# Two filler k-steps in each level of a triangular inverse, set apart (one core, two-layer hybrid encoder step)

## The chip, the cores and the metric

One core of a Trainium2 chip runs the whole program in one launch. The time is the device time of one execution in microseconds (us); the median of three executions is compared. TensorE (PE) multiplies, VectorE (DVE), ScalarE (ACT) and GpSimd (POOL) work beside it, and SyncE (SP) issues the transfers.

## What is computed

Two layers of a streaming encoder over 512 prompt frames and 32 frames of a running stream (544 columns), model width 1024. In each layer one projection of the normalised input gives the columns of three mixers and three gate blocks:

```python
xn = _rms_norm(x, P['norm_mix_pre'][l])
cols = jnp.einsum('btd,dc->btc', xn, P['w_in'][l]).astype(jnp.float32)
ca, cb, cc, cg = _split(cols, [A_COLS, B_COLS, C_COLS, N_BRANCH * D_MODEL])
...
merged = (gates[:, :, 0] * (h_a @ P['w_branch_a'][l])
          + gates[:, :, 1] * (h_b @ P['w_branch_b'][l])
          + gates[:, :, 2] * (h_c @ P['w_branch_c'][l]))
```

A is an mLSTM, B a sliding-window attention, C the RWKV-7 mixer with the recurrence

```python
S = (S * w[:, :, None, :]
     + jnp.einsum('bhij,bhj->bhi', S, -kk)[..., None] * (kk * a)[:, :, None, :]
     + v[..., None] * k[:, :, None, :])
```

A SwiGLU feed-forward layer of width 2816 follows. Everything is in float32.

## The kernel before

**Large products.** All projections are cut into units of 128 output columns (512 KB of weights each, fetched by SyncE into one of three slots). A weight is split into a high part (ScalarE, L1058) and a low part (GpSimd, L1979), the activations likewise, and a k-step of such a unit is three passes of two matmuls over 272 columns; eight k-steps make a unit. The `branch` units are not split: four k-steps of two float32 matmuls. `gate` and `branch` units stand in the plan in turn, eight of each for branch A and eight for branch B while mixer C runs.

**Mixer C** works in five groups: four of 128 frames (two chunks of 64 frames, 8 heads) and one of 32 frames. In each chunk the recurrence becomes matrix products with the inverse of a unit triangular matrix. `c_gram` makes the matrix (a_rb) and the first step of the inverse; then `c_level` doubles the size of the inverted diagonal blocks, five times for L = 64 (k = 1 to 5) and four times for L = 32. It keeps the inverse `inv` (it lies in the buffer `c_scratch`) and its transpose `invT` (in `c_kk`); `w_lev` lies in `c_in_rate`. A level on TensorE is made of these products, each of them 16 small matmuls 64 rows deep (8 of 32 rows in the last group; a float32 matmul leaves two records in the trace):

- W = a_rb times inv, into bank 1 (`psum_mixer<-c_scratch,c_a_rb` in the trace);
- B3, the update of inv, into bank 3 (`psum_mixer<-c_in_rate,c_kk`), left out in the last level;
- B2, the update of invT, into bank 2 (`psum_mixer<-c_kk,c_in_rate`).

VectorE masks W into w_lev (L1553), then subtracts B3 from inv and B2 from invT (both L1561). The waits: B3 needs the mask; the next level's W needs inv updated. `claim` is the wait of TensorE until a bank's last reader is done.

**Filler.** `fill(n)` puts up to n k-steps of the next large unit into TensorE's stream where it would otherwise wait; when the unit is used up it does nothing. The units themselves stand in the plan between the steps of C (`weave`), and take the k-steps that the fillers have left. The other engines walk through the same plan; when a branch product is complete, VectorE multiplies it by its gate and adds it to `merged` (L1764, L1766), in the plan's order, after the updates of the level before it. Every engine does its own list in order, and the order is fixed when the program is written.

The level as TensorE's function has it:

```python
by_head(1, a_rb[:, :, 0, :], inv, ("c_w", l, g, k))
fill(2)
bank[1].claim(pe)
if k < (5 if L == 64 else 4):
    by_head(3, invT, w_lev, ("c_inv", l, g, k))
by_head(2, w_lev, invT, ("c_invT", l, g, k))
```

Of the kernel before, what the change touches and what calls it, by code (L numbers as in the profile page):

```python
# [252 lines left out]
def build(nc, a, o):  # L253
# [166 lines left out]
    with ctx:  # L420
# [29 lines left out]
        def flow(name):  # L450
            if name not in flows:
                flows[name] = count(name)
            return flows[name]
# [87 lines left out]
        def c_group(g):  # L541
            return (P, P * g, 2, 64) if g < 4 else (TS, TP + 1, 1, TS)
# [14 lines left out]
        def _(pe):  # L557
            def mm(out, lhsT, rhs, start=True, stop=True):
                return pe.matmul(out, lhsT, rhs, start=start, stop=stop, skip_group_check=True)  # L559
# [49 lines left out]
            def product(s, steps=8):  # L609

                kind = s[0]
                if kind == "branch":
                    l, b, m = s[1:]
                    rhs = [(acols[:, AQ + k, :], bh[:, k, :], cc[:, k, :])[b] for k in range(4)]
                    gemm(s, rhs=rhs, nk=4, steps=steps)
                else:
                    gemm(s, rh=xh, rl=xl, cut=SPLIT_C if kind == "cols_c" or (kind == "cols_b" and s[2] < 4) else HALF,
                         wait_k=bool(first_user.get("norm")), steps=steps)
                    first_user["norm"] = False

            def fill(steps):

                if unit_at[0] < len(units):
                    s = units[unit_at[0]]
                    if (s[0] in ("cols_b", "cols_c", "gate") or (s[0] == "cols_a" and 12 <= s[2] < 16)
                            or (s[0] == "branch" and s[3] > 0)):
                        product(s, steps)
# [96 lines left out]
            def pairs(c):  # L724

                for p in range(4):
                    for q in range(2):
                        yield 4 * c + p, p, slice(64 * q, 64 * q + 64), slice(64 * q, 64 * q + c_rows[0])
# [31 lines left out]
            def c_level(l, g, k):  # L760


                n, at, nch, L = c_group(g)

                def by_head(b, lhsT, rhs, mark=None):
                    bank[b].claim(pe)
                    for c in range(nch):
                        for i, p, dims, rows in pairs(c):
                            last = mm(mp[b][rows, i * L:(i + 1) * L], lhsT[rows, i, 0:L], rhs[rows, i, 0:L])
                    bank[b].filled(last, "dve", mark)  # L770

                if k == 1:
                    flow("c_inv0").wait_next(pe, "pe")
                else:
                    bank[3].wait_emptied(pe, ("c_inv", l, g, k - 1))
                by_head(1, a_rb[:, :, 0, :], inv, ("c_w", l, g, k))
                fill(2)
                bank[1].claim(pe)
                if k < (5 if L == 64 else 4):
                    by_head(3, invT, w_lev, ("c_inv", l, g, k))  # L780
                by_head(2, w_lev, invT, ("c_invT", l, g, k))

            def c_chain(l, g, c):
# [218 lines left out]
            for s in plan:  # L1002
# [22 lines left out]
                elif kind == "merge_split":  # L1025
                    pass
                elif kind == "mix":
                    gemm(s, rh=xh, rl=xl, wait_k=s[2] == 0)
                elif kind == "ffn_out":
                    l, m, q = s[1:]  # L1030
                    if m == 0 and q == 0:
                        flow("hidden").wait_next(pe, "pe", KF)
                    gemm(s, rh=hid_h, rl=hid_l, k0=8 * q, nk=nk_of(s), first=q == 0, last=q == 2)
                elif kind == "c_shift_out":
                    c_shift_out()
                elif kind == "store_y":
                    pe.wait_ge(flow("x_new").sem, KD * DEPTH)
                    pe.wait_ge(flow("x_new_odd").sem, KD * DEPTH)
                    store_y()
                else:  # L1040
                    {"c_prep": c_prep, "c_gram": c_gram, "c_level": c_level, "c_chain": c_chain, "c_finish": c_finish,
                     "c_state_out": c_state_out, "c_gate_in": lambda l: None, "c_rsqrt": lambda l: None,
                     "c_variance": c_variance,
                     "c_keys": c_keys, "c_scale": c_keys, "c_scaled": c_scaled, "a_norm": lambda l: None,
                     "a_rows": lambda l: None, "a_rows_exp": lambda l: None, "a_rows_put": lambda l: None,
                     "a_rows_get": lambda l: None, "a_scale": lambda l: None, "a_chunk": a_chunk,
                     "a_chunk_out": a_chunk_out, "a_out": a_out, "b_values": b_values, "b_scores": b_scores,
                     "b_out": b_out}[kind](*s[1:])
# [991 lines left out]
```

How the kernel before makes its waits and increments, by code:

```python
    def wait_next(self, eng, who, n=1):  # L120
        self.seen[who] = self.seen.get(who, 0) + n
        eng.wait_ge(self.sem, self.seen[who])
# [8 lines left out]
    def __call__(self, ins, count=None):  # L132
        c = count or self.chain
        c.inc(ins)
        self.eng.wait_ge(c.sem, c.value)
# [12 lines left out]
    def claim(self, pe):  # L148
        if self.last:
            pe.wait_ge(self.empty[self.last].sem, self.full[self.last].value)
# [9 lines left out]
    def wait_emptied(self, eng, mark):  # L161
        eng.wait_ge(*self.marks[mark])
# [397 lines left out]
            def order_after(ins):  # L561
                chains["pe"].inc(ins)
                pe.wait_ge(chains["pe"].sem, chains["pe"].value)
# [3 lines left out]
            def gemm(s, rh=None, rl=None, rhs=None, first=True, last=True, cut=HALF, wait_k=False, k0=0, nk=8, steps=8):  # L568
# [1 line left out]
                ks = range(done_k.get(s, 0), min(nk, done_k.get(s, 0) + steps))
                if not ks:
                    return
                done_k[s] = ks[-1] + 1
                key = s[:3] if s[0] == "ffn_out" else s
                pair, reader, turn = tiles[key]
                if s in split_no:
                    slot = split_no[s] % NSPLIT
                    if ks[0] == 0:
                        pe.wait_ge(low_ready.sem, split_no[s] + 1)
                else:
                    at, value = landed_at[s]
                    slot = unit_no[s] % NRAW
                    if ks[0] == 0:
                        pe.wait_ge(landed[at].sem, value)
                if first and ks[0] == 0 and tile_no[key] >= 2:
```

## Time and profile before

| what | value |
|---|---|
| runs | 2665.5, 2658.36, 2649.56 us, median 2658.36 |
| profiled execution | 2656.14 us; its span, first to last instruction, 2654.4 us |
| PE busy | 2406.3 us (91%), 23176 instructions |
| PE weight loads busy | 2255.5 us (85%) |
| DVE, ACT, POOL busy | 881.6, 845.9, 732.2 us |
| mean granted TensorE clock | 0.952 |
| levels of layer 0 and of layer 1 | between 414 and 723 us, and between 1720 and 2023 us |

The span runs from the first to the last instruction of one execution; the profiled execution's own time is 1.7 us longer. A share of an engine is busy time; the chain of waits tells which busy time set the end. Timeline rows give a start, a duration, the engine, the line (for all small and large products here the helper's line L559), the operation with output and inputs, and how many records are merged; in brackets the idle time before it and who ended it. Durations of matmuls overlap, so that the length of a step is read as the distance from its start to the next step's start.

### The profile page before, as it was taken

How to read it: one execution, taken by the hardware profiler on the slowest of the kernel's cores; microseconds unless marked ns; L12 is line 12 of the kernel's file. 1: busy time of each engine (PE TensorE's matmuls, PEld its weight loads, DVE VectorE, ACT ScalarE, POOL GpSimd, SP SyncE). 2: the span in 40 equal slices, each digit the busy share in tenths (PEclk: the TensorE clock that was granted, in tenths of full speed). 3: DMA queues.
4: the chain of work that ended last, by engine and by line, in shares of the span. 5: the costliest groups of instructions: out<-in, count | busy, mean ns of one | idle time of the engine just before them, and what ended most of it. 6: DMA issues, size and time to landing. Idle time of an engine off the chain costs nothing.

```text
span 2654.4 us, 51984 instructions
## 1 busy us (share of the span) xinstructions
PE 2406.3 (91%) x23176; PEld 2255.5 (85%) x23176; DVE 881.6 (33%) x1394; ACT 845.9 (32%) x1408; POOL 732.2 (28%) x330
## 2 busy tenths in 40 slices
PE   4998898999899799999979889999998988999996
PEld 3997887888798699999969878888887987999996
DVE  2232654554333411110042346454343324111102
ACT  3343441222242422222243344322213243222222
POOL 1321221111122334443333222211102133444342
PEclk9997899999999899999989989999999997999998
DMA  5423210111123133322234231111112131333231
GB/s 153 122 52 68 56 45 26 38 38 37 43 62 117 40 88 88 88 86 80 74 94 118 44 72 49 41 38 38 38 28 63 56 122 40 88 88 88 82 88 56
DMA packets 335447, 181.35 MB, mean 68 GB/s; under 512 B 35512, under 2 KB 332456, under 8 KB 334072
## 3 DMA queue, kind: packets, MB, share of 16 engines
q1 hardware_dynamic: 335224, 178.03, 24.0%
q8 instruction: 183, 3.00, 0.5%
q14 instruction: 40, 0.33, 0.0%
HBM read 168.62 MB, written 9.38 MB: 67 GB/s over the span
## 4 chain that ended last, share of the span: by engine, by line
PE 76%; DVE 9%; ACT 6%; DMA 4%; issue 3%; POOL 2%; SPq 1%; DVEq 0%; ACTq 0%; POOLq 0%
PE psum_products L559 60%; PE psum_mixer L559 15%; DMA w_raw<-in_w_in 2%; POOL w_low L1979 1%; ACT w_high L1058 1%; DVE squares L1422 1%; SPq L1834 1%; DVE x L1438 1%; DMA w_raw<-in_w_out 1%; ACT L1058 1%; DVE squares L1435 1%; DVE squares_ffn L1435 1%; ACT b_scores_even L1058 1%; DMA bias_skewed<-bias_line 0%; DVE a_dexp L1655 0%
## 5 line engine op out<-in xcount | busy, mean ns | idle before, releaser
L1979 POOL TENSOR_TENSOR w_low<-w_raw,w_high 128x1024 fp32r<-128x1024 f32 (+1 forms) x274 | 659.7, 2408 | 1715.9 <-ACT w_high L1058 1715.7
L559 PE MATMUL psum_products<-xn_high,w_high 128*128 128x272 f32 (+2 forms) x3616 | 793.0, 301 | 83.1 <-POOL w_low L1979 38.9
L559 PE MATMUL psum_products<-xn_high,w_low 128*128 128x272 f32 (+2 forms) x3616 | 763.5, 293 | 0.0
L559 PE MATMUL psum_products<-xn_low,w_high 128*128 128x272 f32 (+2 forms) x3616 | 762.5, 293 | 0.0
L559 PEld LDWEIGHTS psum_products<-xn_high,w_high 128*128 128x128 f32 x3616 | 586.4, 194 | 112.2 <-POOL w_low L1979 54.1
L559 PEld LDWEIGHTS psum_products<-xn_low,w_high 128*128 128x128 f32 x3616 | 587.9, 194 | 0.0
L559 PEld LDWEIGHTS psum_products<-xn_high,w_low 128*128 128x128 f32 x3616 | 583.4, 194 | 0.0
L1058 ACT ACTIVATE w_high<-w_raw 128x1024 fp32r<-128x1024 f32 (+1 forms) x274 | 286.5, 1046 | 255.3 <-PE psum_products L559 144.9
L559 PE MATMUL psum_products<-hidden_high,w_high 128*128 128x272 f32 x704 | 147.4, 291 | 4.8 <-DVE hidden_low L1770 4.8
L559 PE MATMUL psum_products<-hidden_low,w_high 128*128 128x272 f32 x704 | 146.4, 289 | 0.0
L559 PE MATMUL psum_products<-hidden_high,w_low 128*128 128x272 f32 x704 | 145.8, 289 | 0.0
L1796 DVE SCALAR_TENSOR_TENSOR ffn_product<-ffn_tanh,psum_products 128x544 f32<-128x544 f32 x44 | 31.7, 721 | 256.9 <-ACT ffn_tanh L1058 256.9
L559 PEld LDWEIGHTS psum_products<-hidden_high,w_high 128*128 128x128 f32 x704 | 111.6, 191 | 5.2 <-DVE hidden_low L1770 5.2
L559 PEld LDWEIGHTS psum_products<-hidden_low,w_high 128*128 128x128 f32 x704 | 111.8, 190 | 0.0
L559 PEld LDWEIGHTS psum_products<-hidden_high,w_low 128*128 128x128 f32 x704 | 111.1, 190 | 0.0
L1058 ACT ACTIVATE hidden_high<-ffn_product 128x544 fp32r<-128x544 f32 x44 | 29.0, 658 | 228.1 <-DVE ffn_product L1803 228.1
L1058 ACT ACT_TABLE_LOAD x69 | 88.5, 1283 | 33.6 <-PE psum_products L559 25.1
L1058 ACT ACTIVATE gate_tanh<-psum_products 128x544 f32<-128x544 f32 x32 | 19.9, 623 | 245.2 <-PE psum_products L559 245.1
L1817 DVE TENSOR_TENSOR squares_ffn<-squares_ffn 128x544 f32<-128x544 f32 x14 | 10.2, 725 | 262.1 <-ACT squares_ffn L1058 262.1
L1803 DVE SCALAR_TENSOR_TENSOR ffn_product<-ffn_product,psum_products 128x544 f32<-128x544 f32 x44 | 31.7, 721 | 174.9 <-PE psum_products L559 174.9
L1655 DVE SCALAR_TENSOR_TENSOR a_dexp<-a_g_spread,a_cols_tokens,consts 128x128 f32<-128x128 f32 (+1 forms) x40 | 31.1, 778 | 150.6 <-ACT stats L1058 149.6
L1058 ACT ACTIVATE ffn_tanh<-psum_products 128x544 f32<-128x544 f32 x44 | 27.5, 624 | 150.1 <-PE psum_products L559 150.1
(311 smaller groups left out, 2643.1 us busy)
## 6 DMA issues: line engine op xcount, KB each, us to landing
w_raw<-in_w_in SPq DMA_DIRECT2D x112, 512.0 KB, 3.8
w_raw<-in_w_ffn_in SPq DMA_DIRECT2D x88, 512.0 KB, 3.7
w_raw<-in_w_ffn_out SPq DMA_DIRECT2D x32, 512.0 KB, 3.4
w_raw<-in_w_out SPq DMA_DIRECT2D x16, 512.0 KB, 3.6
w_raw<-in_w_ffn_out SPq DMA_DIRECT2D x16, 384.0 KB, 3.0
x_kept<-x SPq DMA_DIRECT2D x2, 2176.0 KB, 7.8
x<-x_kept SPq DMA_DIRECT2D x2, 2176.0 KB, 8.5
w_raw<-in_w_in SPq DMA_DIRECT2D x16, 256.0 KB, 3.2
```

What stands on the lines that cost most here:

```text
L559: return pe.matmul(out, lhsT, rhs, start=start, stop=stop, skip_group_check=True)
L1058: return act.activation(out, in_, f, **kw_)
L1422: step(stt(out=squares[:, k, :], in0=x[:, k, :], scalar=prm[:, l, g0 + k:g0 + k + 1], in1=rstd[:], op0=MUL, op1=MUL), xn_part)
L1435: step(stt(out=tmp[:, k, :], in0=src[:, k, :], scalar=prm[:, l, g0 + k:g0 + k + 1], in1=rstd[:], op0=MUL, op1=MUL), flow("x_step_odd") if ...
L1438: step(tt(x[:, k, :], x[:, k, :], tmp[:, k, :], ADD), flow("x_new"))
L1655: step(stt(out=dexp[0:n, h * n:(h + 1) * n], in0=g_all[0:n, h, at:at + n], scalar=a_cols_t[0:n, g, h:h + 1], in1=C("future_neg")[0:n, 0:n] ...
L1796: step(stt(out=halves(ffn_p[:, j % 2, :]), in0=halves(ffn_t[:, j % 2, :]), scalar=1.0, in1=pair_view(pair), op0=ADD, op1=MUL), emptied["dve"])
L1803: step(stt(out=halves(ffn_p[:, j % 2, :]), in0=halves(ffn_p[:, j % 2, :]), scalar=0.5, in1=pair_view(pair), op0=MUL, op1=MUL), emptied["dve"])
L1817: step(tt(sq[:, 0, :], sq[:, 0, :], sq[:, m, :], ADD), flow("squares_added") if m == KD - 1 else None)
L1834: c.inc(sp.dma_start(dst, src), 16)
L1979: low_ready.inc(pool.tensor_tensor(wl[:, n % NSPLIT, 0:nk], wraw[:, slot, 0:nk], wh[:, n % NSPLIT, 0:nk].bitcast(F32), ALU.subtract))
```

## The change

In `c_level` on TensorE the two k-steps no longer stand together behind W: one stays there, the other goes between B3 and B2. The wait for bank 1 (the mask) stays between the first k-step and B3; in the last level, which has no B3, it now stands between the two k-steps.

```diff
@@ -774,10 +774,11 @@
                 else:
                     bank[3].wait_emptied(pe, ("c_inv", l, g, k - 1))
                 by_head(1, a_rb[:, :, 0, :], inv, ("c_w", l, g, k))
-                fill(2)
+                fill(1)
                 bank[1].claim(pe)
                 if k < (5 if L == 64 else 4):
                     by_head(3, invT, w_lev, ("c_inv", l, g, k))
+                fill(1)
                 by_head(2, w_lev, invT, ("c_invT", l, g, k))
```

The order of the other four engines is the same, row for row. Per layer there are 24 levels: in 16 the filler is parted (the 13 at full width are 7 with gate k-steps and 6 with branch k-steps; the 3 of the 32-frame group have gate k-steps), in 5 (the last of each group) the wait falls between the two k-steps, and in 3 the unit is used up and there is no filler.

TensorE's order, group 0 of layer 0, first level; the filler is a gate unit (`psum_products<-xn_high,w_high` and its two companions). Before:

```order
L559 MATMUL psum_mixer<-c_scratch,c_a_rb 64x64 [waits bank1_emptied_by_dve,c_inv0]
L559 MATMUL psum_mixer<-c_scratch,c_a_rb 64x64 x15
L559 MATMUL psum_products<-xn_high,w_high 128x272 x2
L559 MATMUL psum_products<-xn_low,w_high 128x272 x2
L559 MATMUL psum_products<-xn_high,w_low 128x272 x2
L559 MATMUL psum_products<-xn_high,w_high 128x272 x2
L559 MATMUL psum_products<-xn_low,w_high 128x272 x2
L559 MATMUL psum_products<-xn_high,w_low 128x272 x2
L559 MATMUL psum_mixer<-c_in_rate,c_kk 64x64 [waits bank3_emptied_by_dve,bank1_emptied_by_dve]
L559 MATMUL psum_mixer<-c_in_rate,c_kk 64x64 x15
L559 MATMUL psum_mixer<-c_kk,c_in_rate 64x64 [waits bank2_emptied_by_dve]
L559 MATMUL psum_mixer<-c_kk,c_in_rate 64x64 x15
```

The same place in the changed kernel:

```order
L559 MATMUL psum_mixer<-c_scratch,c_a_rb 64x64 [waits bank1_emptied_by_dve,c_inv0]
L559 MATMUL psum_mixer<-c_scratch,c_a_rb 64x64 x15
L559 MATMUL psum_products<-xn_high,w_high 128x272 x2
L559 MATMUL psum_products<-xn_low,w_high 128x272 x2
L559 MATMUL psum_products<-xn_high,w_low 128x272 x2
L559 MATMUL psum_mixer<-c_in_rate,c_kk 64x64 [waits bank3_emptied_by_dve,bank1_emptied_by_dve]
L559 MATMUL psum_mixer<-c_in_rate,c_kk 64x64 x15
L559 MATMUL psum_products<-xn_high,w_high 128x272 x2
L559 MATMUL psum_products<-xn_low,w_high 128x272 x2
L559 MATMUL psum_products<-xn_high,w_low 128x272 x2
L559 MATMUL psum_mixer<-c_kk,c_in_rate 64x64 [waits bank2_emptied_by_dve]
L559 MATMUL psum_mixer<-c_kk,c_in_rate 64x64 x15
```

Three rows (six matmuls, one k-step) have moved from ahead of B3 to behind it. The last level of the same group, before:

```order
L559 MATMUL psum_products<-xn_high,w_high 128x272 [waits products_emptied_by_act,w_low_ready]
L559 MATMUL psum_products<-xn_high,w_high 128x272
L559 MATMUL psum_products<-xn_low,w_high 128x272 x2
L559 MATMUL psum_products<-xn_high,w_low 128x272 x2
L559 MATMUL psum_products<-xn_high,w_high 128x272 x2
L559 MATMUL psum_products<-xn_low,w_high 128x272 x2
L559 MATMUL psum_products<-xn_high,w_low 128x272 x2
L559 MATMUL psum_mixer<-c_kk,c_in_rate 64x64 [waits bank2_emptied_by_dve,bank1_emptied_by_dve]
```

And in the changed kernel:

```order
L559 MATMUL psum_products<-xn_high,w_high 128x272 [waits products_emptied_by_act,w_low_ready]
L559 MATMUL psum_products<-xn_high,w_high 128x272
L559 MATMUL psum_products<-xn_low,w_high 128x272 x2
L559 MATMUL psum_products<-xn_high,w_low 128x272 x2
L559 MATMUL psum_products<-xn_high,w_high 128x272 [waits bank1_emptied_by_dve]
L559 MATMUL psum_products<-xn_high,w_high 128x272
L559 MATMUL psum_products<-xn_low,w_high 128x272 x2
L559 MATMUL psum_products<-xn_high,w_low 128x272 x2
L559 MATMUL psum_mixer<-c_kk,c_in_rate 64x64 [waits bank2_emptied_by_dve]
```

Here no matmul has moved; the wait for the mask has moved ahead of the second k-step.

## Rows read from the trace of the kernel before

**Rows 1.** Chain of waits, shares of the span by line

```profile
PE psum_products L559 60%; PE psum_mixer L559 15%; DMA w_raw<-in_w_in 2%; POOL w_low L1979 1%; ACT w_high L1058 1%; DVE squares L1422 1%; SPq L1834 1%; DVE x L1438 1%; DMA w_raw<-in_w_out 1%; ACT L1058 1%; DVE squares L1435 1%; DVE squares_ffn L1435 1%; ACT b_scores_even L1058 1%; DMA bias_skewed<-bias_line 0%; DVE a_dexp L1655 0%
```

**Rows 2.** Windows: length, busy PE, PEld, DVE, ACT, POOL; PEclk; DMA share; GB/s

```profile
380.00:720.00 340.00, 312.67 (x4926) 278.30 (x4925) 154.63 (x255) 90.66 (x154) 48.72 (x25) 0.97 0.14 39
1680.00:2040.00 360.00, 332.94 (x5181) 295.54 (x5180) 164.24 (x277) 95.99 (x163) 52.80 (x27) 0.97 0.15 39
414.00:440.00 26.00, 24.59 (x520) 22.01 (x518) 10.39 (x16) 1.68 (x2) 2.35 (x1) 1.00 0.12 33
```

**Rows 3.** Timeline, group 0, first level, gate filler: start, length, engine, operation

```profile
414.31 1.15 PE L559 MATMUL psum_mixer<-c_scratch,c_a_rb 64*64 64x64 f32 x32
415.39 0.52 PE L559 MATMUL psum_products<-xn_high,w_high 128*128 128x272 f32 x2
415.58 0.69 DVE L1553 TENSOR_TENSOR c_in_rate<-psum_mixer,consts 128x512 f32<-128x512 f32 x1 [1.92 <-PE psum_mixer L559]
...
417.09 1.15 PE L559 MATMUL psum_mixer<-c_in_rate,c_kk 64*64 64x64 f32 x32
...
419.10 0.52 PE L559 MATMUL psum_products<-xn_high,w_high 128*128 128x272 f32 x2
...
420.80 1.15 PE L559 MATMUL psum_mixer<-c_scratch,c_a_rb 64*64 64x64 f32 x32
```

**Rows 4.** Timeline, group 0, second level, branch filler, up to the next W

```profile
423.91 1.15 PE L559 MATMUL psum_mixer<-c_in_rate,c_kk 64*64 64x64 f32 x32
424.89 1.10 PE L559 MATMUL psum_mixer<-c_kk,c_in_rate 64*64 64x64 f32 x32
425.18 0.69 DVE L1561 TENSOR_TENSOR c_scratch<-c_scratch,psum_mixer 128x512 f32<-128x512 f32 x1 [2.42 <-PE psum_mixer L559]
425.92 1.15 PE L559 MATMUL psum_mixer<-c_scratch,c_a_rb 64*64 64x64 f32 x32
```

**Rows 5.** Timeline of c_gram: one k-step alone, gate and branch

```profile
409.02 0.52 PE L559 MATMUL psum_products<-xn_high,w_high 128*128 128x272 f32 x2
...
409.97 1.96 PE L559 MATMUL psum_mixer<-c_kappa_r,c_kprime 64*64 64x128 f32 x32
...
633.16 1.19 PE L559 MATMUL psum_products<-b_heads,w_raw 128*128 128x272 f32 x4
...
634.27 1.96 PE L559 MATMUL psum_mixer<-c_kappa_r,c_kprime 64*64 64x128 f32 x32
```

**Rows 6.** Timeline, group 0, fourth level, no filler left

```profile
431.04 1.15 PE L559 MATMUL psum_mixer<-c_scratch,c_a_rb 64*64 64x64 f32 x32
...
433.05 1.15 PE L559 MATMUL psum_mixer<-c_in_rate,c_kk 64*64 64x64 f32 x32 [0.86 <-DVE c_in_rate L1553]
```

**Rows 7.** Timeline, group 1, fourth level, two merge operations ahead of the mask

```profile
505.79 1.15 PE L559 MATMUL psum_mixer<-c_scratch,c_a_rb 64*64 64x64 f32 x32
...
506.70 0.72 DVE L1764 SCALAR_TENSOR_TENSOR gate_product<-gate_tanh,psum_products 128x544 f32<-128x544 f32 x1
...
508.21 0.69 DVE L1553 TENSOR_TENSOR c_in_rate<-psum_mixer,consts 128x512 f32<-128x512 f32 x1
508.96 1.15 PE L559 MATMUL psum_mixer<-c_in_rate,c_kk 64*64 64x64 f32 x32 [0.33 <-DVE c_in_rate L1553]
```

**Rows 8.** Timeline, group 0, last level: W and its mask

```profile
435.06 1.15 PE L559 MATMUL psum_mixer<-c_scratch,c_a_rb 64*64 64x64 f32 x32
...
436.73 0.69 DVE L1553 TENSOR_TENSOR c_in_rate<-psum_mixer,consts 128x512 f32<-128x512 f32 x1
```

**Rows 9.** Timeline, group 4 (32 frames): B3, next W, its mask, next B3

```profile
713.84 0.44 PE L559 MATMUL psum_mixer<-c_in_rate,c_kk 32*32 32x32 f32 x16
...
715.05 0.44 PE L559 MATMUL psum_mixer<-c_scratch,c_a_rb 32*32 32x32 f32 x16 [0.52 <-DVE c_scratch L1561]
...
715.66 0.60 DVE L1553 TENSOR_TENSOR c_in_rate<-psum_mixer,consts 32x128 f32<-32x128 f32 x2
...
717.12 0.44 PE L559 MATMUL psum_mixer<-c_in_rate,c_kk 32*32 32x32 f32 x16
```

## The prediction

> **What bounds the kernel now.** I read the chain of waits first, then the windows over the two stretches in which the levels run, then the timeline of single levels. The chain ends in TensorE for three quarters of the span: matmuls into psum_products 60%, into psum_mixer 15% [rows 1]. So whatever lengthens TensorE's own stream there lengthens the kernel, unless a wait that is timed by something else absorbs it. In both stretches TensorE is busy 92% of the time at a mean granted clock of 0.97, and inside the levels at 1.00 [rows 2].
>
> A level has three products, called W, B3 and B2 here (banks 1, 3, 2). On VectorE a mask follows W, and the updates of inv and invT follow B3 and B2. The timeline of group 0 gives all prices of a full-width level [rows 3, 4]:
> - W holds TensorE 1.08 us when filler follows (414.31 to 415.39).
> - Two gate k-steps in one piece take 1.70 (415.39 to 417.09); two branch k-steps 2.03 (3.11 from 420.80 to 423.91, less 1.08).
> - B3 takes 0.98 when B2 follows (423.91 to 424.89), and B2 1.03; together 2.01, from B3 to the next W or to the next product.
> - The inv update ends at 425.87, 0.05 before W at 425.92. By its spacing W could have come some 0.1 earlier, so this is the whole wait that a filler between B3 and B2 can hide at full width.
> - The first wait is the larger one. Where no filler is left, B3 comes 2.01 after W, 0.86 of it idle until the mask is done [rows 6]. With one k-step of filler W's side is 1.08 + 0.95 = 2.03: it just covers the mask. The second k-step is spare there, which is the case for moving it.
>
> **What the change costs.** No instruction is added or removed; VectorE, ScalarE, GpSimd and the DMA queue keep their order. On TensorE one of two k-steps moves from ahead of B3 to behind it in 16 levels of a layer (13 at full width, 3 in the narrow group 4). In the five last levels, which have no B3, both k-steps stay together and the wait for the mask is now ahead of the second. In three levels the filler has run out and nothing changes.
>
> A split filler is dearer than a whole one. A single gate k-step between two small products takes 0.95 (409.02 to 409.97), a single branch k-step 1.11 (633.16 to 634.27) [rows 5]. So two apart cost 1.90 against 1.70, or 2.22 against 2.03, and B3, now followed by filler, 1.08 instead of 0.98: 0.30 us for each place where 64-row and 128-row matmuls alternate once more. The Trainium skill (TensorEngine Tiling (Array Packing), Key Properties) says that going to another tiling mode drains the engine, while another tile of the same mode doesn't; it gives no figure. By that rule the charge falls on every split level and on no last level; without it the sum below would be 4.4 us instead of 14.0, which is the first rival. The trace's lone k-steps agree with it, but none of them stands between B3 and B2.
>
> Per layer, in us:
> - Gate level straight into the next W: before 1.08 + 1.70 + 2.01 = 4.79, after 1.08 + 0.95 + 1.08 + 0.95 + 0.98 = 5.04: +0.25 (the 0.05 is the wait gained). Two of these: +0.50. Branch level likewise 5.12 to 5.36: +0.24, six: +1.44.
> - Gate level with a gate product behind it: B2 takes 1.08 too, and there was no wait to gain: +0.35, two: +0.70.
> - Levels in which the mask is late. VectorE has two merge operations of a finished branch product (L1764, L1766) ahead of the mask, which starts 2.42 after W instead of 1.26; B3 starts 3.17 after W [rows 7]. Before, the two k-steps ran inside that time and only 0.33 stood idle. Now the first k-step ends at 2.03, TensorE idles 1.14, B3 starts where it did, and the whole moved piece comes on top: 3.01 instead of 2.01 from B3 on, +1.00. Two: +2.00. What is queued behind the idle TensorE is the spare filler itself; nobody else waits. One further level has a single merge operation ahead of its mask, which then ends 2.36 after W (as in [rows 8]): B3 at 2.42 instead of 2.78, then +1.00: +0.64.
> - Last levels. The first k-step is through at 1.94, the mask at about 2.01: 0.08 idle, and restarting costs about 0.11, half of the 0.20 by which a lone k-step (0.95) exceeds a following one (1.70 less 0.95): +0.19, two. In group 0 the mask comes at 2.42 [rows 8]: +0.59. In group 3 the filler is a branch, +0.10. Sum +1.07.
> - Group 4 (32 rows wide). W takes 0.37 (2.07 to B3 less 1.70 of filler), its mask starts 0.61 after it and takes 0.60, W then stood 1.21 behind B3, 0.52 of it idle until inv was updated [rows 9]. Here the filler does hide the wait: the middle level goes from 2.07 + 1.21 = 3.28 to about 1.49 (the mask waits for the invT update ahead of it, and one k-step no longer covers it) + 1.60 (0.37 + 0.95 + 0.28) = 3.09, -0.20. In the first a merge operation delays the mask, so W's side stays and only 1.21 becomes 1.60 (+0.39); the third has a gate product behind it and no wait to lose (2.07 + 0.63 to 1.49 + 1.69, +0.48); the last is covered. +0.67.
>
> Together 0.50 + 1.44 + 0.70 + 2.00 + 0.64 + 1.07 + 0.67 = 7.02 per layer, 14.0 us for both. After the levels TensorE waits for ScalarE (the next group's tanh) and for w_low, but those chains begin with work that TensorE itself finishes behind the levels, so they move along and absorb nothing.
>
> The profiled execution took 2656.1 (span 2654.4), so its counterpart takes 2670.1; against the median of 2658.4, which is 2.2 above it, **2672**. No row shows the new place itself. Bounds: from below 4.4 (no charge for the change of shape), from above 16.6 (0.05 more for each of 32 split levels, 0.1 for each of 10 last ones). I take the lone k-steps at face value, since the small products on both sides are of the same form as B3 and B2.
>
> **Rivals.**
> 1. The charge for changing shape is already paid once in a level, and a further filler costs only its matmuls. Then 0.30 x 32 = 9.6 goes and 4.4 remains (the late masks and the last levels, 5.6, less what the narrow and the plain levels then gain): 2663. For it: the weight loads are the same ones either way. Against: both lone rows, gate and branch, show the surcharge.
> 2. Not slower: the clock. The two stretches run at 0.97 over 700 us, so up to 21 us go to the lower of TensorE's two levels (1.2 instead of 2.4 GHz), outside the levels [rows 2]. The change alters how long each level lasts and so what the clock meets in the preparations between the groups. If most of these dips fell away (19 us), the result is 2653; it turns the sign when more than 14 of the 21 come back. Against: the dips stand at waits that the change leaves as they are. Its rule in the Trainium skill (TensorE: Matmul & The Clock Gate, Part 1) is that the slow clock is the default and activity releases it; the change adds no matmul, and by it I would expect no gain.
> 3. The same thing the other way round: in the late levels TensorE now idles 1.14 instead of 0.33, and if the clock halves for one level's length (5 us at the high level) behind each of those four, four times 2.5 us are added: some 2682.
> 4. The change does nothing measurable because the spare k-step was hidden work anyway. The order speaks against it: the k-step keeps its length wherever it stands, and the only idle time in which it could vanish is the 0.1 of inv at full width and the 0.52 of the narrow levels [rows 4, 9].
>
> **How the numbers follow.** The sum as worked out, +11 to +17: 0.62. Rival 1: 0.17. Rival 2: 0.06, rival 3: 0.08, rest 0.07. The three runs of before spread over 16 us, and about 0.5% (13.3 us) is what a measurement of this kernel can tell from no change. The sum lies just above that bound, so I give the forecast's 0.62 as 0.39 beyond and 0.23 within; rivals 1 and most of 2 are within, rival 3 is beyond. Slower by over 0.5%: 0.50; within: 0.45; faster: 0.05. The range takes in rival 1 partly and 12 us to either side for the spread: 2660 to 2684.
>
> **What would show it.** In the profile after, the first level's B3 starts 2.03 behind W, the k-step behind it takes 0.95, and the next W comes about 3 us behind B3 where it had come 2.01. TensorE's waits for the mask (c_in_rate) grow from single gaps of 0.86 and 0.33 to 1.1 in the late levels, its wait for c_scratch vanishes in the narrow group, and group 0's five levels last 1.4 longer. The prediction is wrong if a split level lasts no longer than 4.79, if the mean clock moves by more than 0.005, or if a wait further on shrinks by what the levels gain in length.

## The result, and the profile after

Over 13 runs of each kernel the ratio is 1.0033 with a 95% interval of 1.0019 to 1.0047, so the change costs 8.7 us (5 to 12.5). The medians, 2652.65 and 2664.91 us, lie further apart, 12.3 us, and the means 8.3; every cost below is a ratio less one, times the median of before. Repeated beside the kernel before in a later session (among the experiments below) the ratio was 1.0035 (1.0020 to 1.0051), 9.3 us, with medians 11.0 apart. The forecast was slower by 14.0 us, beyond 0.5%, with a chance of 0.50; the measured cost lies within 0.5%. The profiled execution took 2656.46 us (span 2654.7), at a mean granted clock of 0.959 instead of 0.952. It happens to lie 6 us under the mean of its kernel's runs, so it is no longer than that of before, and only its parts can be compared.

The chain of waits after, by line. TensorE still sets the end, and the masks (c_in_rate, L1554) now have a share of their own:

```profile
PE psum_products L559 59%; PE psum_mixer L559 15%; DMA w_raw<-in_w_in 2%; POOL w_low L1980 1%; ACT w_high L1059 1%; DVE squares L1423 1%; SPq L1835 1%; DVE x L1439 1%; DMA w_raw<-in_w_out 1%; ACT L1059 1%; DVE squares_ffn L1436 1%; DVE squares L1436 1%; DVE c_in_rate L1554 1%; ACT b_scores_even L1059 1%; DMA bias_skewed<-bias_line 0%
```

The waits of TensorE on VectorE's masks, in total, times, longest: first before, then after.

```profile
PE psum_mixer L559 <- DVE c_in_rate L1553: 6.8, 12, 0.9
PE psum_mixer L559 <- DVE c_scratch L1561: 2.1, 4, 0.5
```

```profile
PE psum_mixer L559 <- DVE c_in_rate L1554: 13.0, 18, 1.1
PE psum_products L559 <- DVE c_in_rate L1554: 0.6, 2, 0.3
```

The wait for the mask has doubled (6.8 to 13.0 + 0.6), the wait for inv (c_scratch, L1561; L1562 after) has gone. That is the exchange which the change makes: 2.1 us gained against 6.8 lost, before any price for alternating.

The timeline of group 0, first level, and the start of the recurrence behind the five levels (answers to [rows 3]):

```profile
418.12 1.15 PE L559 MATMUL psum_mixer<-c_scratch,c_a_rb 64*64 64x64 f32 x32
419.19 0.52 PE L559 MATMUL psum_products<-xn_high,w_high 128*128 128x272 f32 x2
...
420.14 1.15 PE L559 MATMUL psum_mixer<-c_in_rate,c_kk 64*64 64x64 f32 x32
421.22 0.52 PE L559 MATMUL psum_products<-xn_high,w_high 128*128 128x272 f32 x2
...
422.18 1.15 PE L559 MATMUL psum_mixer<-c_kk,c_in_rate 64*64 64x64 f32 x32
423.25 0.52 PE L559 MATMUL psum_products<-xn_high,w_high 128*128 128x272 f32 x2
...
424.95 1.15 PE L559 MATMUL psum_mixer<-c_scratch,c_a_rb 64*64 64x64 f32 x32
...
443.95 0.63 PE L559 MATMUL psum_mixer<-c_v_tokens,c_b_rk 64*64 64x64 f32 x16
```

W to B3 takes 2.02, the k-step between B3 and B2 0.96, B3 itself 1.08: each as priced from the lone k-steps of [rows 5]. From the first W to the chain it is 25.83 us (443.95 less 418.12); before, 24.52 (the chain began at 438.83, [rows 3] has W at 414.31).

Group 1, fourth level, the late mask (answers to [rows 7]):

```profile
511.35 1.15 PE L559 MATMUL psum_mixer<-c_scratch,c_a_rb 64*64 64x64 f32 x32
...
512.26 0.72 DVE L1765 SCALAR_TENSOR_TENSOR gate_product<-gate_tanh,psum_products 128x544 f32<-128x544 f32 x1
...
513.78 0.69 DVE L1554 TENSOR_TENSOR c_in_rate<-psum_mixer,consts 128x512 f32<-128x512 f32 x1
514.52 1.15 PE L559 MATMUL psum_mixer<-c_in_rate,c_kk 64*64 64x64 f32 x32 [1.07 <-DVE c_in_rate L1554]
...
517.53 1.10 PE L559 MATMUL psum_mixer<-c_scratch,c_a_rb 64*64 64x64 f32 x32
```

B3 comes 3.17 after W as before, idle time is 1.07 instead of 0.33, and W follows 3.01 behind B3: the moved k-step comes wholly on top.

Group 4 (answers to [rows 9]):

```profile
717.36 0.42 PE L559 MATMUL psum_mixer<-c_scratch,c_a_rb 32*32 32x32 f32 x16
...
718.27 0.60 DVE L1554 TENSOR_TENSOR c_in_rate<-psum_mixer,consts 32x128 f32<-32x128 f32 x2
718.93 0.44 PE L559 MATMUL psum_mixer<-c_in_rate,c_kk 32*32 32x32 f32 x16 [0.20 <-DVE c_in_rate L1554]
...
720.53 0.42 PE L559 MATMUL psum_mixer<-c_scratch,c_a_rb 32*32 32x32 f32 x16
```

The wait of 0.52 for inv is gone; one k-step no longer covers the mask (0.20 idle). The level takes 3.17 instead of 3.28.

Adding up the distances from each group's first W to its chain (in group 4 to the transposed state at the chain's head): 111.6 us per layer before, 118.3 after (in both layers, to 0.05 us). **The levels are 6.7 us per layer longer, 13.4 for both, where the forecast had 7.02 and 14.0.** By the two ratios 4 to 5 us of that are missing in the time (0.9 to 8.4 by the first interval, up to 8.1 and down to nothing by the second); if so, they came back outside the levels. The windows over the two stretches give the direction (340 and 360 us before at 0.97, [rows 2]):

```profile
380.00:725.00 345.00, 316.82 (x4925) 277.47 (x4924) 155.56 (x257) 90.36 (x153) 48.45 (x25) 0.98 0.14 38
1680.00:2045.00 365.00, 334.04 (x5165) 292.05 (x5164) 162.86 (x275) 95.56 (x161) 53.17 (x27) 0.98 0.14 39
```

The preparation of a group runs from its first product with the tanh to its first W. That of group 3, first before, then after, with TensorE's wait for w_low inside it:

```profile
601.55 1.13 PE L559 MATMUL psum_mixer<-c_tanh_w,lora 64*128 64x128 f32 x8 [0.98 <-ACT c_tanh_w L1058]
...
618.05 0.82 PE L559 MATMUL psum_products<-xn_high,w_high 128*128 128x272 f32 x2 [2.19 <-POOL w_low L1979]
...
637.28 1.15 PE L559 MATMUL psum_mixer<-c_scratch,c_a_rb 64*64 64x64 f32 x32
```

```profile
611.33 1.13 PE L559 MATMUL psum_mixer<-c_tanh_w,lora 64*128 64x128 f32 x8 [0.98 <-ACT c_tanh_w L1059]
...
627.82 0.52 PE L559 MATMUL psum_products<-xn_high,w_high 128*128 128x272 f32 x2 [2.19 <-POOL w_low L1980]
...
645.53 1.15 PE L559 MATMUL psum_mixer<-c_scratch,c_a_rb 64*64 64x64 f32 x32
```

The windows around that wait, first before:

```profile
616.00:618.00 2.00, 0.00 (x0) 0.00 (x0) 0.00 (x0) 1.97 (x3) 2.00 (x2) 1.00 0.45 99
618.00:622.00 4.00, 3.95 (x19) 3.95 (x20) 2.24 (x4) 3.43 (x5) 1.05 (x2) 0.57 0.49 147
622.00:628.00 6.00, 6.00 (x41) 5.39 (x39) 4.24 (x6) 1.68 (x2) 1.86 (x2) 1.00 0.00 0
```

and after:

```profile
625.60:627.60 2.00, 0.02 (x1) 0.00 (x0) 0.00 (x0) 1.97 (x3) 2.00 (x1) 1.00 0.38 77
627.60:631.60 4.00, 3.79 (x30) 3.79 (x31) 2.08 (x3) 3.61 (x5) 1.17 (x2) 1.00 0.53 158
```

TensorE had stood idle for the same 2.19 us in both. Before, the granted clock then fell to 0.57 over the next 4 us (that is the lower level, 1.2 of 2.4 GHz, for most of them), and it got through 19 matmul records where it now got through 30. Such a fall costs 1.5 us: the preparation of group 3 lasts 35.73 and 35.46 us in the two layers before, and 34.20 and 33.94 after (in the second layer behind 1.92 us of idle time in both).

This is one place of many. By the clock records of the two traces the lower level costs 128 us of the execution before and 108 of the one after; only 15 and 12 of these lie between the first preparation and the last level of the two layers. So the two profiled executions do not show where the missing time came back.

### The profile page after: what moved, and what is told of

The parts are those of the page before. It is cut to its first block, busy times and chain, and to the rows that moved or that the text cites. A ratio compares the mean times of both kernels' runs of the same rounds, so it can differ in the third digit from the quotient of the medians.

```text
span 2654.7 us, 51974 instructions
## 1 busy us (share of the span) xinstructions
PE 2399.0 (90%) x23176; PEld 2240.6 (84%) x23176; DVE 888.0 (33%) x1394; ACT 846.2 (32%) x1408; POOL 733.1 (28%) x330
## 4 chain that ended last, share of the span: by engine, by line
PE 75%; DVE 10%; ACT 6%; DMA 4%; issue 3%; POOL 2%; SPq 1%; DVEq 0%; ACTq 0%; POOLq 0%
PE psum_products L559 59%; PE psum_mixer L559 15%; DMA w_raw<-in_w_in 2%; POOL w_low L1980 1%; ACT w_high L1059 1%; DVE squares L1423 1%; SPq L1835 1%; DVE x L1439 1%; DMA w_raw<-in_w_out 1%; ACT L1059 1%; DVE squares_ffn L1436 1%; DVE squares L1436 1%; DVE c_in_rate L1554 1%; ACT b_scores_even L1059 1%; DMA bias_skewed<-bias_line 0%
## 5 line engine op out<-in xcount | busy, mean ns | idle before, releaser
L559 PE MATMUL psum_products<-xn_high,w_high 128*128 128x272 f32 (+2 forms) x3616 | 791.3, 301 | 85.2 <-POOL w_low L1980 39.1
```

## The experiments

Eleven kernels in three sessions, each session on one chip and beside the kernel before; the text takes them by session: the first four tell apart whether the levels' length reaches the time whole (Theory A) or in part (Theory B), the next four what the missing part hangs on (Theory C), the last three whether longer levels alone bring it back (Theory D) or only parted filler does (Theory E). The last column is the mean granted clock of a kernel's runs; the kernel before had 0.9520, 0.9524 and 0.9517 in the three (29, 31 and 23 runs), and beside the first row its clock is not on record. A level length is read from the timeline as above, both layers summed, against before.

| kernel | levels, us | measured, us (95%) | mean clock |
|---|---|---|---|
| changed, first | +13.4 | +8.7 (5.0 to 12.5) | 0.9572 |
| changed, again | +13.4 | +9.3 (5.3 to 13.6) | 0.9546 |
| last levels back | +11.5 | +6.7 (2.7 to 10.9) | 0.9552 |
| alternation only | +12.6 | +7.7 (2.9 to 12.2) | 0.9549 |
| both behind B3 | +45.6 | +41.5 (34 to 49) | 0.9488 |
| W, four repeated | +9.1 | +6.4 (2.9 to 9.9) | 0.9535 |
| W, ten repeated | +27.7 | +22.9 (18.4 to 27.4) | 0.9568 |
| changed, masks first | +5.5 | +6.4 (4.3 to 8.8) | 0.9523 |
| before, masks first | -2.2 | -2.4 (-5.6 to +0.8) | 0.9517 |
| one k-step, masks first | -3.4 | +3.2 (-1.3 to +7.4) | 0.9508 |
| one k-step at full width | -4.5 | -2.7 (-5.6 to +0.3) | 0.9518 |
| before, again | 0 | +1.6 (-2.4 to +5.9) | 0.9514 |

**The kernel before as a kernel of its own** (no edit): how far a ratio strays by itself, and its clock.

> The kernel before, timed as a kernel of its own. The traces show the 24 levels of a layer 6.7 us longer in the changed kernel (13.5 us for both layers), while the measured difference is 8.7 us (5 to 12). Theory A: the levels' 13.5 us enter the time in full, and what the granted clock does elsewhere is chance of the single run; then this kernel runs at the same mean clock as the changed one (0.957 in its runs), and ratio 1.000 against before. Theory B: a kernel with longer levels is granted a somewhat higher clock elsewhere and gets a third of the time back; then this one's runs show a mean clock 0.003 to 0.005 below the changed kernel's 0.957.

Measured 1.0006 (0.9991 to 1.0022), mean clock 0.9514 over 12 runs. Within one kernel a run with a clock 0.001 higher is some 0.7 to 1.8 us shorter (slopes within the kernels of the three sessions), so 0.003 to 0.005 more clock is worth about 2 to 9 us: what is missing fits in. The clock is 0.006 below the 0.957 of the changed kernel's runs in another session, where Theory B expected 0.003 to 0.005; beside each other, further down, the two kernels differ by 0.002. Theory B's first half (a higher clock in the changed kernel) holds in its direction.

**Both k-steps behind B3**:

```diff
-                fill(2)
+                last_level = k == (5 if L == 64 else 4)
+                fill(2 if last_level else 0)
                 bank[1].claim(pe)
-                if k < (5 if L == 64 else 4):
+                if not last_level:
                     by_head(3, invT, w_lev, ("c_inv", l, g, k))
+                    fill(2)
                 by_head(2, w_lev, invT, ("c_invT", l, g, k))
```

> Both k-steps of a level go between B3 and B2, none behind W (the last levels keep both behind W). W's wait for the mask is then bare (2.01 us at full width, 0.86 of it idle), and B3 to the next W takes 1.08 + 1.70 + 0.98. Per layer: eight plain levels +0.98, two with a product behind +1.08, two with the late mask +1.75, one +1.39, three narrow ones +3.0 together: 17.9, for both layers +36 us. Theory A: +33 to +38 us against before. Theory B (a third given back by the clock): +21 to +26 us and a mean clock above that of the kernel before by 0.01. Were the charge for alternating shapes absent (rival 1 of the prediction), 0.30 less in each of 32 levels: no, since here the number of alternations is that of before; the mask wait alone decides.

Measured 1.0156 (1.0129 to 1.0183), +41.5 us. "A third is given back" is refuted: nothing proportional comes back. The bare waits are as expected, and the late mask leaves 2.02 us idle; timeline of group 3:

```profile
652.13 1.15 PE L559 MATMUL psum_mixer<-c_in_rate,c_kk 64*64 64x64 f32 x32 [0.86 <-DVE c_in_rate L1555]
...
657.31 1.15 PE L559 MATMUL psum_mixer<-c_in_rate,c_kk 64*64 64x64 f32 x32 [2.02 <-DVE c_in_rate L1555]
```

The levels grew by 45.6 instead of 36 us, because here the clock falls inside them too: group 4's levels took 20.7 us at a granted clock of 0.75, where some 17 were expected. The mean clock of the runs, 0.9488, is the lowest of all.

**The alternation of shapes alone**: between the two k-steps behind W, two 64 by 64 matmuls on a constant, in the levels with a B3.

```diff
-                fill(2)
+                last_level = k == (5 if L == 64 else 4)
+                fill(2 if last_level else 1)
+                if not last_level and unit_at[0] < len(units) and 0 < done_k.get(units[unit_at[0]], 0):
+                    s_ = units[unit_at[0]]
+                    if done_k[s_] < nk_of(s_):
...
+                            mm(gp[r_, 2 * pair_ + _q, 300:364], C("eye64")[r_], C("eye64")[r_])
+                        fill(1)
```

> The kernel before, with two 64 by 64 matmuls on the constant unit matrix, written to columns of the product bank that nobody reads, between the two k-steps behind W in the levels with a B3. No wait loses cover; only the shape alternates once more. If each alternation costs what the lone k-steps showed (0.20, and 0.10 at the small ones, plus some 0.1 for the two matmuls): +0.4 in ten plain full-width levels, little in the three with a late mask (idle time hides it), +0.35 in three narrow ones: 5 us a layer, +10 us for both, and the level 2.78 from W to B3 becomes 3.15 to 3.25. If alternating is free: +0.1 per level, +3 us. Theory B takes a third off either.

The kernel adds these matmuls to the computation. Measured 1.0029 (1.0011 to 1.0046), +7.7 us; the trace, first level of group 0:

```profile
421.31 1.15 PE L559 MATMUL psum_mixer<-c_scratch,c_a_rb 64*64 64x64 f32 x32
422.39 0.52 PE L559 MATMUL psum_products<-xn_high,w_high 128*128 128x272 f32 x2
423.34 0.33 PE L559 MATMUL psum_products<-consts 64*64 64x64 f32 x4
423.60 0.52 PE L559 MATMUL psum_products<-xn_high,w_high 128*128 128x272 f32 x2
424.55 1.15 PE L559 MATMUL psum_mixer<-c_in_rate,c_kk 64*64 64x64 f32 x32
```

Each k-step takes 0.95 once it stands alone (422.39 to 423.34, 423.60 to 424.55), 1.90 for the two instead of 1.70, and the two small matmuls 0.26: W to B3 is 3.24 instead of 2.78. The small matmuls write to psum_products like the filler itself, and no wait loses its cover, so the surcharge comes with the change of shape, and rival 1 falls.

**The last levels back**:

```diff
-                fill(1)
+                last_level = k == (5 if L == 64 else 4)
+                fill(2 if last_level else 1)
                 bank[1].claim(pe)
...
+                if not last_level:
                     by_head(3, invT, w_lev, ("c_inv", l, g, k))
-                fill(1)
+                    fill(1)
```

> The changed kernel, with the last level of each group as before (both k-steps ahead of the wait for the mask). The last levels cost 0.57, 0.14, 0.14, 0.02 and 0 us per layer in the profile after, so 1.8 us for both layers go: +11.7 us of levels against before by the traces. Theory A: +10 to +13 us measured. Theory B: +7 to +8 us.

Levels 117.3 per layer, 1.0 us less than in the changed kernel; measured 1.0025 (1.0010 to 1.0041), +6.7. This is Theory B's figure; whether a third (3.8 us) or some 5 us are missing cannot be told at this size, and it is the kernel with both k-steps behind B3 that speaks against a third. The mean clock was 0.9552.

**The changed kernel again** (no edit).

> The changed kernel once more, now beside the kernel before on one chip, with the clock of every run. Its levels are 13.4 us longer by the trace. Theory A (the levels' sum enters in full): +11 to +16 us. Theory C (the time outside the levels is about 5 us shorter, since the granted clock falls less often in the preparations between the groups): +7 to +10 us and a mean clock 0.003 to 0.005 above that of the runs of before beside it.

Measured 1.0035 (1.0020 to 1.0051), and a mean clock of 0.9546 against 0.9524. This is Theory C's figure, though its interval still touches 13.4.

**Masks first**, on the changed kernel and on the kernel before: VectorE's `branch` merges wait until the next level's mask is issued.

```diff
                     step(tt(w_lev[r, 0:ni, 0:L], by_head(1, r), level_mask(k, r, ni, L), MUL),
                          bank[1].empty["dve"] if r is rows[-1] else None)
+                while late_merges:
+                    branch(late_merges.pop(0))
...
                 elif kind == "branch":
-                    branch(s)
+                    rest = [i[0] for i in plan[at_ + 1:at_ + 4] if i[0] != "gate"]
+                    if rest and rest[0] == "c_level":
+                        late_merges.append(s)
+                    else:
+                        branch(s)
```

> The changed kernel, and VectorE masks W before it merges a finished branch product, instead of after. Then no mask is late: per layer 1.07 us of idle time goes in two levels, 0.45 in one, 0.4 in group 0's last and 0.9 in the first narrow one, 3.9 together, 7.8 us for both layers; the levels end 5.6 us above before. The merges then delay the update of inv by some 0.2 us, which the filler behind B3 hides. Theory A: +4 to +7 us against before. Theory C: -2 to +2 us. If the late masks were not a cost of the change (the idle time would be made up elsewhere), nothing moves against the changed kernel: +9 us.

> The kernel before, and VectorE masks W before it merges. Here the k-steps already hid most of the late masks: per layer 0.39 us twice and 0.2 in the narrow group, less 0.2 in each of three levels where the merges now delay inv: 0.4 us a layer, -1 us for both. Theory A: 0 to -2 us. Theory C, in the form that any shift of the groups against each other spares clock: -4 to -7 us.

On the changed kernel the late mask is gone; group 1, fourth level:

```profile
512.58 1.15 PE L559 MATMUL psum_mixer<-c_scratch,c_a_rb 64*64 64x64 f32 x32
...
513.84 0.69 DVE L1554 TENSOR_TENSOR c_in_rate<-psum_mixer,consts 128x512 f32<-128x512 f32 x1 [0.39 <-PE psum_mixer L559]
514.57 0.72 DVE L1767 SCALAR_TENSOR_TENSOR gate_product<-gate_tanh,psum_products 128x544 f32<-128x544 f32 x1
514.60 1.15 PE L559 MATMUL psum_mixer<-c_in_rate,c_kk 64*64 64x64 f32 x32
```

B3 follows W by 2.02 instead of 3.17. The levels fell to 114.4 per layer, 7.9 us off both layers (7.8 expected), which is what the late masks cost the changed kernel. Yet the time stayed at +6.4 (4.3 to 8.8), with a clock of 0.9523, the same as before's: nothing came back here. Theory C in its general form is refuted. On the kernel before the same edit gives -2.2 us of levels, so 5.7 us of the change's 13.4 are late masks that it made dearer and 7.7 are not; it measured 0.9991 (0.9979 to 1.0003), clock 0.9517: no difference that can be told from none, and Theory C's -4 to -7 is wrong in its middle.

**One k-step per level**, masks first: `fill(2)` becomes `fill(1)`; then the same with two in the narrow and last levels (`fill(1 if L == 64 and k < 5 else 2)`).

> One k-step behind W and none between B3 and B2, masks first: the filler lasts for 23 of the 24 levels instead of 21, and one k-step (2.03 us with W) covers the mask (2.01). A level of full width without filler costs 0.73 us more of idle time than one with, so two of them save 1.5 us a layer; the masks 0.4 more: the levels, counted without their filler, are 1.9 us a layer shorter than before, -4 us for both layers. Theory A: -3 to -5 us. Theory C: -7 to -10 us. The narrow levels lose 0.2 each, within that.

Measured 1.0012 (0.9995 to 1.0028), a miss: about +3 us. The levels are 3.4 us shorter, but the chains behind them, which now hold more of the filler, are 6.3 us longer (130.5 instead of 124.2 from each chain's start to the next group's tanh product). And group 4's levels took 17.1 and 16.1 us instead of 14.0, with a clock of 0.70 in the first layer:

```profile
711.40:728.50 17.10, 15.91 (x228) 14.12 (x228) 7.17 (x23) 1.56 (x2) 0.00 (x0) 0.70 0.24 63
```

> Masks first, and one k-step behind W in the levels of full width that have a B3; the last levels and the narrow group keep two. In the kernel with one k-step everywhere the narrow levels ran at the low clock (17.2 and 16.1 us instead of 14.0), which this avoids. The filler lasts for 23 of 24 levels, worth 0.73 us in two levels of a layer, and masks first gave 1.1 us a layer by the trace: 2.5 us a layer, -5 us for both. If k-steps left over for the chains and the plan's own units cost as much as they did there (3 us more in the chains of a layer), the result is 0 to -2 us.

Measured 0.9990 (0.9979 to 1.0001). The levels with less filler are 4.5 us shorter and the chains 1.5 us longer; the interval does not exclude no gain. Neither of the two versions can be said to beat the kernel before. Of the three masks-first kernels without parted filler two lie on the faster side (-2.4 and -2.7 us) and one on the slower (+3.2).

**Longer levels by plain matmul time**: some of W's small matmuls issued twice, to the same place (4, then 10 of 16).

```diff
-                        for i, p, dims, rows in pairs(c):
+                        for r_, (i, p, dims, rows) in enumerate(list(pairs(c))[:4 // nch if b == 1 else 0] + list(pairs(c))):
```

> The kernel before, with four (two in the narrow group) of W's sixteen small matmuls issued twice, to the same place: levels longer by pure matmul time, filler where it was, no new idle time and no new alternation. 0.058 us each: +0.23 us in some 18 levels and +0.12 in four: 4.5 us a layer, +9 us for both layers. Theory A (the levels' length enters in full): +8 to +10 us. Theory D (once a layer's levels are some 5 us longer, whatever makes them so, the clock falls less often in the preparations of groups 3 and 4 and 4 to 5 us come back): +4 to +6 us. Theory E (what comes back belongs to filler that is parted or covered less): +8 to +10 us, the preparation of group 3 at 35.5 us as before, not at 34.2.

> The same with ten of sixteen (five in the narrow group): +0.58 us in some 18 levels, 11 to 12 us a layer, +23 us for both. Theory A and Theory E: +21 to +25 us. Theory D: +17 to +20 us, and the preparation of group 3 takes 34.2 us instead of 35.5.

With four the levels grew by 9.1 us, and 1.0024 (1.0011 to 1.0037) was measured, 6.4 us; the preparation of group 3 took 34.21 and 33.95 us. The total lies between the theories and its interval holds both, the preparation speaks against Theory E. With ten the levels grew by 27.7 us (0.069 per matmul, dearer than the 0.058 assumed), and 1.0086 (1.0069 to 1.0103), 22.9 us, was measured, at a clock of 0.9568. The 22.9 lies in the range that was given for Theories A and E and above that of Theory D, but these ranges were worked out for levels 23 us longer; against the 27.7 that they grew by, 4.8 us came back with the filler just where it was. The interval (18.4 to 27.4) leaves 27.7 just outside, and all but one of the six runs have a higher clock than every run of the kernel before. This speaks against Theory E: a part comes back without parted filler and without new idle time. The preparation of group 3 took 35.76 and 33.94 us, so the 34.2 foretold for it came in one layer only. Theory D is supported by the times of five kernels, but loosely: the changed kernel with masks first, 2.8 us a layer longer, got nothing back, and four repeats, at 4.5, got 2.7 us back (6.2 at most).

The ten preparations of an execution, added up from the timelines, separate the kernels better than group 3's alone, though not wholly. They take 325.6, 331.9 and 328.6 us in the profiles of before, before again and before with masks first, and 327.5 and 327.3 in the two with one k-step. In the eight profiles of kernels with longer levels they take 319.8 to 326.0 (322.9 and 321.3 in the two of the changed kernel). The changed kernel with masks first is among these, at 322.9, although its time got nothing back. And outside mixer C single executions differ by more than that: from layer 0's last level to layer 1's first tanh product the thirteen profiles took 957.8 to 968.6 us.

## Why the prediction was wrong in size

- **The bound**: right. TensorE's chain set the end, and the levels' length went into the time.
- **Two k-steps apart cost more than two together**: right, 0.95 each and 1.08 for B3, and the alternation alone shows it. The Trainium skill (TensorEngine Tiling (Array Packing), Key Properties: changing the tiling mode drains the engine) points the same way; the timelines put 0.30 us on one further alternation. That it is a drain no row shows.
- **Late masks +1.00 each**: right (3.17 + 3.01), and removing their cause took 7.9 us off the levels.
- **Last levels +1.07 per layer**: right; putting them back took 1.0 off.
- **Plain levels +0.25 and +0.24**: 0.04 to 0.06 too high each. W after a B2 that stood behind filler takes 1.03, not 1.08 (from 517.53 to the k-step at 518.56 in the timeline after). A gate level (group 2's fourth, 586.36 to 591.34) took 4.98 where 5.04 was worked out, and a branch level (group 0's third, 430.32 to 435.64) 5.32 instead of 5.36. Over a layer the full-width groups grew by 5.9 us where 6.35 had been worked out.
- **Group 4, +0.67 per layer**: measured +0.83 (14.79 instead of 13.96); its middle level gained 0.11 (3.28 to 3.17), not 0.20.
- **The sum of the levels**: 14.0 forecast, 13.4 measured.
- **The step that failed** is the one behind the sum: "so they move along and absorb nothing". The waits did move along unshortened: TensorE's wait for ScalarE's tanh is 13.3 us in both profiles, for w_low 38.9 and 39.1. But not everything behind the levels kept its length: 8.7 and 9.3 us were measured where the levels grew by 13.4, so that some 4 to 5 us were given back elsewhere, and the granted clock rose with it (0.9546 against 0.9524 side by side; 0.959 against 0.952 in the profiles, beyond the 0.005 that the prediction had named as a sign of being wrong). Group 3's preparation, 1.5 us shorter in each layer, is one place where this can be seen. The prediction had this as its second rival, with a chance of 0.06 and as an all-or-nothing case that changes the sign; a partial return, which leaves the sign and moves the time across the 0.5% bound, was in none of its cases. The reason given against it ("the change adds no matmul, and by it I would expect no gain") looked at the amount of work. The rule of the Trainium skill cited there (TensorE: Matmul & The Clock Gate, Part 1) names activity as what releases the clock; here the same idle 2.19 us, with the same work around it, was once followed by the low clock and once not. The ten repeats say that longer levels by themselves can bring such a return.
- **The base**: the forecast's 2672 stood on a median of three runs, 2658.4; 13 runs give 2652.65. The measured 2664.9 lies in the range.

**What stays open.** Why the clock is higher, and where the time comes back. In the six layers of three profiles (before, its repeat, and before with masks first) the preparation of group 3 took 35.4 to 35.7 us, in the four of the changed kernel 33.9 to 34.2. But it does not go by the levels' length alone: with one k-step at full width, whose levels are shorter than before's, it took 34.23 and 35.47, the same as with both k-steps behind B3 (34.20 and 35.47), whose levels are the longest. In the preparations of groups 0, 1 and 2 both kernels have falls in some layers and none in others. That points to when the idle time comes rather than to how long it is, but no run here moved one idle period by a known amount and nothing else. The interval of most single comparisons also leaves room for a return of 0 to 9 us, and by the medians the changed kernel's two comparisons have only 1.1 and 2.4 us missing. It is the agreement of the changed kernel's two sessions and of four other kernels (4.1 to 4.9 us each, three of them against the same runs of the kernel before), and, but for the one with both k-steps behind B3, the clock of their runs, that makes the 4 to 5.

## What to carry to other kernels

Filler between two products should fill exactly the wait that is there: one piece more than a wait needs is not spare if the wait is sometimes longer (here a late mask), and a piece cut in two pays for each further change of matmul shape. Read both from the trace before moving: how long the wait is in its worst instance, and what a lone piece costs where one already stands alone. And a cost summed on the bound engine's timeline, however exact, still passes through the clock: with a mean granted clock below 1, a change of 0.5% can lose a part of itself there (here about a third, with an interval from nearly nothing to well over half), so the range should reach to a partial return.

## What was not expected of the hardware

- After the same idle 2.19 us of TensorE, the granted clock fell to its lower level in the kernel before (0.57 over 4 us, 1.5 us lost) and stayed at 1.00 in the changed one.
- Five of the kernels with longer levels ran at a mean clock 0.002 to 0.005 above before's (0.9535 to 0.9572 against 0.9517 to 0.9524). The changed kernel with masks first did not (0.9523), nor did the one in which TensorE stood idle inside the levels most (0.9488).
- In the 32-row levels with a single k-step of filler the clock was 0.70 over 17 us and 0.79 over 16; with two it was at 1.00 and the same levels took 14.0 us.
- Two further 64 by 64 matmuls between 128-row ones took 0.26 us, against 0.06 each in a row of sixteen.
